# RWKV-7 scan on one NeuronCore: every product of the chunked scan in a 64x64 cell of the array

## The reference

```python
def step(s, inp):
    r_t, w_t, k_t, v_t, a_t, b_t = inp
    sa = jnp.einsum('bhij,bhj->bhi', s, a_t)
    s = s * w_t[:, :, None, :] + sa[..., None] * b_t[:, :, None, :] + v_t[..., None] * k_t[:, :, None, :]
    return s, jnp.einsum('bhij,bhj->bhi', s, r_t)
```

## Time and profile before

| | |
|---|---|
| median of three runs | 2237.53 us |
| profiled execution, span | 2236.4 us |
| PE, PEld busy | 2129.4 us (95%), 1368.9 us (61%) |
| DVE, ACT, POOL busy | 1177.5 (53%), 774.6 (35%), 647.4 us (29%) |
| granted TensorE clock, mean | 0.983 |

### The profile page before, as it was taken

How to read it: one execution, slowest core, us unless ns; L and a number is a source line. 1 busy time by engine, 2 the same in 40 slices (tenths; PEclk the granted TensorE clock), 3 DMA queues, 4 the chain that set the end, 5 groups by cost and what they waited for, 6 DMA issues and landing times. The chain is left out here.

```text
span 2236.4 us, 56049 instructions
## 1 busy us (share of the span) xinstructions
PE 2129.4 (95%) x23756; PEld 1368.9 (61%) x23756; DVE 1177.5 (53%) x2284; ACT 774.6 (35%) x2065; POOL 647.4 (29%) x901
## 2 busy tenths in 40 slices
PE   7999999999999999999896999999999999999798
PEld 3556565354444455444345888888888888888443
DVE  5443343134946770042624666666666666666674
ACT  4111111143255522210113444444444444444332
POOL 1010010023033410011123545444545444444011
PEclk9999999999999999999997999999999999999899
DMA  9201003701037766555314334533333333333742
GB/s 353 79 19 38 19 19 122 273 29 38 31 95 191 208 167 188 163 169 195 127 57 123 91 95 119 139 92 94 93 93 92 97 90 101 86 102 73 231 118 110
DMA packets 315866, 258.17 MB, mean 115 GB/s; under 512 B 138849, under 2 KB 272225, under 8 KB 312162
## 3 DMA queue, kind: packets, MB, share of 16 engines
q1 hardware_dynamic: 315618, 254.59, 37.9%
HBM read 174.80 MB, written 79.69 MB: 114 GB/s over the span
## 5 line engine op out<-in xcount | busy, mean ns | idle before, releaser
L1019 PE MATMUL ps<-xt,w_slab 128*128 128x512 f32 (+1 forms) x800 | 297.5, 526 | 0.0
L2168 PE MATMUL ps<-M,AT 64*64 64x64 f32 x6400 | 264.2, 224 | 7.6 <-ACT M L1957 4.4
L1883 POOL TENSOR_TENSOR SP<-Q,decay 64x128 f32<-64x128 f32 x304 | 128.7, 423 | 428.1 <-DVE Q L2086 399.6
L2168 PEld LDWEIGHTS ps<-M,AT 64*64 64x64 f32 x6400 | 219.3, 135 | 46.5 <-issue 14.6
L1019 PEld LDWEIGHTS ps<-xt,w_slab 128*128 128x128 f32 x800 | 148.3, 190 | 146.3 <-issue 122.6
L2168 PE MATMUL ps<-TT,MT 64*64 64x64 f32 x5120 | 215.6, 223 | 8.5 <-DVE TT L2029 1.3
L2168 PEld LDWEIGHTS ps<-TT,MT 64*64 64x64 f32 x5120 | 178.0, 135 | 39.6 <-issue 30.3
L2029 DVE COPY_PREDICATED TT<-mask,ps 128x128 f32<-128x128 int32 x400 | 125.1, 319 | 91.0 <-PE ps L2168 85.3
L2075 DVE STREAM_TRANSPOSE MT<-M 128x256 f32<-128x256 f32 x240 | 106.1, 442 | 125.8 <-ACT M L1957 123.8
L2161 PE MATMUL ps<-ar,bk 64*128 64x192 f32 (+1 forms) x1280 | 142.4, 342 | 14.3 <-POOL ar L1901 14.3
L645 PE MATMUL ps<-h,fgo 128*128 128x512 f32 x320 | 141.6, 597 | 2.4 <-PEq L202 2.4
(11 more groups left out here) (291 smaller groups left out, 3592.3 us busy)
## 6 DMA issues: line engine op xcount, KB each, us to landing
feat<-feature_scratch SPq DMA_DIRECT2D x160, 256.0 KB, 3.2
feature_scratch<-k_feats SPq DMA_DIRECT2D x64, 320.0 KB, 5.2
feature_scratch<-k_feats SPq DMA_DIRECT2D x24, 640.0 KB, 6.8
k_feats<-in_modw SPq DMA_DIRECT2D x8, 1536.0 KB, 6.7
w_slab<-in_rwin SPq DMA_DIRECT2D x24, 512.0 KB, 6.9
Q<-v_token_scratch SPq DMA_DIRECT2D x320, 32.0 KB, 2.5
Z<-v_token_scratch SPq DMA_DIRECT2D x320, 32.0 KB, 2.4
fgo<-in_modw SPq DMA_DIRECT2D x8, 1024.0 KB, 8.2
```

The source lines that it names most:

```text
L1019: mm = pe.matmul(ps[:, bank, 0:n], (w1t if i is None else w[:, i % 2])[:, k, :], src[:, k, a:a + n], start=k == 0, stop=k == KT - 1)
L1883: g.tensor_tensor(SP[own(h)], turn(sub, Q[l][own(h), h]), pend_turn(c, own(h), sub).unsqueeze(2).broadcast_to([HD, NDIR, CK]), ALU.mult).t ...
L2168: mm = pe.matmul(out[o, b, :], L[o, b, :], R[o, b, :], start=True, stop=True)
```

## The change

The reference's arithmetic stays. Every matmul of the scan becomes 64 rows by 64 columns. A cell whose rows and columns belong to one head is an "own" place; one whose rows are of one head and whose columns (output partitions) are of the other is a "crossed" place. The array has two of each.

- `products`: for each block four matmuls, two own (keys b against a, identity, r: tile `NG`, bank 0) and two crossed (keys k against the same: tile `XG`, bank 1), instead of two of 128 columns. ScalarE copies the own part (`first_n`), VectorE masks the crossed part (`first_x`) and the r columns (`first_r`), once per direction; products(1) waits for the copies of products(0).
- The values' products (`v_of_a`, `v_of_k`, `v_of_r`) run on the crossed places, for the following half-step, placed between the own matmuls of `a_state`, `r_state` and `sa`; the own products add onto them in PSUM later (`start=False`).
- Values are loaded four times a chunk rather than eight, into one tile V; the state has its own tile S; GpSimd scales and VectorE adds it in one instruction of 128 partitions rather than two of 64. GpSimd writes the a operand once instead of twice.
- The lists are reordered: TensorE does a_state, r_state, m4, products(0), sa, t8, b_state, y, m8, products(1), a_state, r_state, t16, sa, t2, m16, b_state, y, m2, t32, t4, mt32. On ScalarE the copy of sa(1) now stands behind that of m16, and the copy of products(0) ahead of that of sa(0).

```diff
-    RBK, BKt, Q, Z = ([sb(f"{n}{l}", [P, 2, B4, CK]) for l in range(SETS)] for n in ("RBK", "BKt", "Q", "Z"))
+    ar, NG, XG = ([sb(f"{n}{l}", [P, B4, 3, CK]) for l in range(SETS)] for n in ("ar", "NG", "XG"))
+    V = [sb(f"V{l}", [P, B4, CK]) for l in range(SETS)]
...
+            def first_n(j, cc, d):
+                act.wait_ge(pa, count("first", j, cc, PA[f"g{d}"]))
+                act.activation(gout(NG[lng(cc)], d, 0, 2), gall(0, 0, 2), ACT.Copy).then_inc(aa, 1)
...
+                if A_:
+                    first_n(j, c + 2, 0)
                 if Q_:
                     sa(j, c, 0)
-                if A_:
-                    first_at(j, c + 2)
                 if B_:
                     second(j, c + 1, "m8")
                 if A_:
-                    first_bk(j, c + 2)
+                    first_n(j, c + 2, 1)
                 if Q_ and is_lat(c):
                     y(j, c, 0)
                 if Q_:
                     r(j, c, 1)
-                    sa(j, c, 1)
                 if B_:
                     second(j, c + 1, "m16")
+                if Q_:
+                    sa(j, c, 1)
+                if A_:
+                    first_m2(j, c + 2)
...
+            def first_x(j, cc, d):
+                n = 3 if is_lat(cc) else 2
+                v.wait_ge(pa, count("first", j, cc, PA[f"g{d}"]))
+                v.tensor_tensor(gout(XG[lng(cc)], d, 0, n), gall(1, 0, n), xmask[d][:, 0:n * CK].unsqueeze(1).broadcast_to([P, 2, n * CK]), ALU.mult).then_inc(da, 1)
+
+            def first_r(j, cc, d):
+                v.wait_ge(aa, count("act_first", j, cc, AA[f"n{d}"]))
...
             def products(j, cc, d):
...
+                else:
+                    pe.wait_ge(aa, count("act_first", j, cc, AA["n0"]))
+                    pe.wait_ge(da, count("dve_first", j, cc, DA["x0"]))
...
                     for h in two:
                         o = own(h)
-                        mm = pe.matmul(gp(h, d, b)[:, cols[h], :], bk[s][o, 2 * d + b, :, :], ar[l][o, 2 * d + b, cols[h], :], start=True, stop=True)
+                        pe.matmul(gp(o, 0, b, n), bk[s][o, i, h, :], ar[l][o, i, 0:n, :], start=True, stop=True)
+                    for h in two:
+                        o = own(h)
+                        mm = pe.matmul(gp(other(h), 1, b, n), bk[s][o, i, 1 - h, :], ar[l][o, i, 0:n, :], start=True, stop=True)
...
+            def v_of_a(j, nx, d):
+                c, sub = nx
+                i = at(sub, d)
+                for h in two:
+                    pe.matmul(chain(sub, "r")[own(h), d, :], XG[lng(c)][other(h), i, 0, :], V[lng(c)][other(h), i, :], start=d == 0, stop=False, skip_group_check=True)
...
+            def a_state(j, c, sub):
+                nx = following(j, c, sub)
+                pe.wait_ge(dst, count("two", j, c, sub) + 1)
...
+                for d in range(NDIR):
+                    for h in two:
+                        o = own(h)
+                        mm = pe.matmul(chain(sub, "r")[o, d, :], ar[lng(c)][o, at(sub, d), 0, :], S[sub][o, d, :], start=False, stop=True, skip_group_check=True)
+                    if nx:
+                        v_of_a(j, nx, d)
                 mm.then_inc(pr, 1)
...
+            def b_state(j, c, sub):
+                pe.wait_ge(asa, count("two", j, c, sub + 1))
+                if not has_state((c, sub)):
+                    return
                 for d, h in pairs:
                     o = own(h)
+                    mm = pe.matmul(chain(sub, "st")[o, d, :], NG[lng(c)][o, at(sub, d), 1, :], SA[sub][o, d, :], start=False, stop=True, skip_group_check=True)
                 mm.then_inc(pst, 1)
```

More of the change, by code:

```diff
@@ L1878, in state_scaled @@
                 l = lng(c)
[L1879 to L1885, removed]
+                g.wait_ge(dst, count("two", j, c, sub) + 1)
+                g.tensor_tensor(SP[:], S[sub][:], pend_turn(c, slice(0, P), sub).unsqueeze(2).broadcast_to([P, NDIR, CK]), ALU.mult).then_inc(sp_ready, 1)
             def operands(j, cc):
@@ L2016, in _ @@
             v.wait_ge(tab_in, 16)
-            for h in two:
-                v.memset(turn(0, Q[0][own(h), h]), 0.0).then_inc(dst, 1)
+            v.memset(S[0][:], 0.0).then_inc(dst, 1)
             def masks():
@@ L2046, in first_m1 @@
                 v.transpose(flat(M[s]), flat(MT1[s][:])).then_inc(da, 1)
[L2048 to L2059, removed]
+            def first_x(j, cc, d):
[4 more added lines that the diff above has]
+                v.wait_ge(aa, count("act_first", j, cc, AA[f"n{d}"]))
+                v.tensor_tensor(gout(NG[lng(cc)], d, 2, 3), gall(0, 2, 3), xmask[d][:, 128:192].unsqueeze(1).broadcast_to([P, 2, CK]), ALU.mult).then_inc(drm, 1)
             def first_t(j, cc, k):
@@ L2205, in mt32, with following @@
                 pe.wait_ge(db, count("dve_second", j, cc, DB["t32"]))
-                level(lev(5), TT[32][s], MT[s], pb)
+                level(lev(5), TT[32][s], MT[trd(j, cc)], pb)
             def at(sub, d):
                 return 2 * d + (sub if d == 0 else 1 - sub)
-            def r(j, c, sub):
-                l = lng(c)
-                pe.wait_ge(dst, count("four", j, c, 2 * sub) + 2)
+            def following(j, c, sub):
                 if sub == 0:
-                    pe.wait_ge(ld_v[l], j * 256 + 128 + c // SETS * 128)
-                    pe.wait_ge(da, count("dve_first", j, c, DA["ak1"]))
-                for d, h in pairs:
-                    mm = pe.matmul(seq(6)[own(h), d, :], ar[l][:, at(sub, d), 3 * h, :], Q[l][:, h, at(sub, d), :], start=True, stop=True)
-                mm.then_inc(pr, 1)
+                    return (c, 1)
+                return (c + 1, 0) if j < KT - 1 or c + 1 < NCH else None
@@ new lines, in v_of_a, with v_of_k @@
+            def v_of_a(j, nx, d):
[3 more added lines that the diff above has]
+                    pe.matmul(chain(sub, "r")[own(h), d, :], XG[lng(c)][other(h), i, 0, :], V[lng(c)][other(h), i, :], start=d == 0, stop=False, skip_group_check=True)
+            def v_of_k(j, nx, d):
+                c, sub = nx
+                i = at(sub, d)
+                for h in two:
+                    mm = pe.matmul(chain(sub, "st")[own(h), d, :], XG[lng(c)][other(h), i, 1, :], V[lng(c)][other(h), i, :], start=False, stop=False, skip_group_check=True)
+                return mm
@@ new lines, in v_of_r, with v_ready, has_state @@
+            def v_of_r(j, nx, d):
+                c, sub = nx
+                i = at(sub, d)
+                for h in two:
+                    pe.matmul(ybank(sub)[own(h), d, :], XG[lng(c)][other(h), i, 2, :], V[lng(c)][other(h), i, :], start=d == 0, stop=False, skip_group_check=True)
+            def v_ready(j, cc):
+                pe.wait_ge(ld_v[lng(cc)], j * 128 + (cc // NCH * 128 + 64 + cc % NCH // SETS * 64))
+                pe.wait_ge(da, count("dve_first", j, cc, DA["x1"]))
+            def has_state(nx):
+                return nx != (NCH - 1, 1)
@@ L2221, in sa, with r_state @@
+            def r_state(j, c, sub):
+                nx = following(j, c, sub)
+                for d in range(NDIR):
+                    if is_lat(c):
+                        for h in two:
+                            o = own(h)
+                            pe.matmul(ybank(sub)[o, d, :], ar[lng(c)][o, at(sub, d), 2, :], S[sub][o, d, :], start=False, stop=False, skip_group_check=True)
+                    if nx and has_state(nx):
+                        v_of_k(j, nx, d)
             def sa(j, c, sub):
+                nx = following(j, c, sub)
@@ L2224, in sa @@
                     pe.wait_ge(ab, count("act_second", j, c, AB["xt"]))
-                ge(pe, ay, count("y", j, c, sub if is_lat(c) else 0))
+                ride = nx and is_lat(nx[0])
+                if ride:
+                    last = nx[0] - 1
+                    ge(pe, ay, count("y", j, last, nx[1] + 1 if is_lat(last) else 0))
+                for d in range(NDIR):
+                    for h in two:
+                        o = own(h)
+                        mm = pe.matmul(chain(sub, "sa")[o, d, :], MT[trd(j, c)][o, at(sub, d), :], Rs[sub][o, d, :], start=False, stop=True, skip_group_check=True)
+                    if ride:
+                        v_of_r(j, nx, d)
@@ L2250, in y @@
-            def y(j, c, sub):
-                l = lng(c)
-                for d, h in pairs:
-                    mm = pe.matmul(seq(7)[own(h), d, :], RBK[l][:, h, at(sub, d), :], Z[l][:, h, at(sub, d), :], start=False, stop=True, skip_group_check=True)
+                    mm = pe.matmul(ybank(sub)[o, d, :], NG[lng(c)][o, at(sub, d), 2, :], SA[sub][o, d, :], start=False, stop=True, skip_group_check=True)
                 mm.then_inc(py, 1)
@@ L2260, in period @@
                 if Q_:
-                    r(j, c, 0)
+                    a_state(j, c, 0)
+                    r_state(j, c, 0)
                 if B_:
```

197 lines of the change are left out of this document (94 added, 103 removed).

## The result

The changed kernel takes 2224.06 us (median of 6 runs) against 2237.35 us for the kernel before on the same chip: ratio 0.9947, 95% interval 0.9928 to 0.9965, so 13 us less (8 to 16). The direction was forecast; the size was not: 39 us were forecast. The profiled execution has a span of 2221.9 us, 14.5 less than before.

A forecast was written before the change was run, and what follows sets the result against it. TensorE was taken as the bound: the latent period falls from 11.24 to 10.65 us (8.29 matmuls plus 2.36 waits and stops). 28 us from 48 periods and 11 from 32 give 2198 us; range 2135 to 2250.

The forecast's parts named there:

- Shapes: TensorE, latent period: with all cells 64x64, twelve shape changes of 0.15 us go, 1.80 us less.
- Four places at no cost: TensorE: crossed products run beside own ones, adding 0 us per latent period, between bounds of 0 and 2.68.
- Rival A: TensorE: own and crossed places of the same rows take turns; latent period 12.19 us, total 2309, slower; chance 10%.
- Waits up to sa(1): Latent period walked from a_state at 0 to sa(1) at 5.59 to 5.87 us, with waits at m4 and b_state.
- the two waits of b_state: TensorE idles before b_state for sa's copy on ScalarE: 0.35 us in the first half, 0.70 in the second.
- B: ScalarE's copies queue at full length without overlap; latent period 11.43 us, total 2253; chance 12%.
- C: Shape-change drains go and waits stay at 1.15 us; latent period 9.44, total 2103; chance 8%.
- mt1 5.30, m1 0.44 later for 0.45: t2 starts at 6.24: VectorE's chain ahead of TensorE's t2: m1 follows mt1, so t2 starts at 6.24 us after a 0.37 wait.
- At nothing. GpSimd loses instructions: GpSimd's part was taken to cost nothing: it works a period ahead at under half load.
- 28 were forecast: Gain over the 48 periods with c = 2 to 7, like the one walked: 0.58 us each, 28 us.
- the 32 periods that were not walked: Periods that touch the context, mean before 10.71 us; 11 us of gain taken for them.
- The 0.35 for the others: Gain per period for the 32 not walked: the middle between 0.1 and 0.58 us.

The follow-up runs named there:

- e5: Changed kernel with products put back into cells of 64 rows by 128 columns (one head's data wrong): latent period 10.88 us.
- e4: Changed kernel without the 24 value products on the crossed places (values' part left out of the result): 2215.7 us, latent period 10.86.
- e3: Changed kernel with sa(1)'s copy on ScalarE ahead of m16's copy, as in the kernel before: 2182.50 us, latent period 10.11.
- e2: Changed kernel with GpSimd's list reordered so that no operand product runs beside mt1: 28 us gained, latent period 10.63.
- e7: Changed kernel with NG by kind, GpSimd's operand products kept off mt1, and several ScalarE and VectorE copies moved ahead: 2172 us.
- e8: e7 with the last projection's weights loaded in 64 pieces over all head pairs: 6 us off e7, 0.968 of the kernel before.
- e11: e3 with the crossed value products all issued but moving one column instead of 64: 2181.75 us.

## Why the prediction was wrong

- **Shapes: right.** No gap of 0.15 is left; 0.85 became 0.65 at products, and e5 brings 0.85 back.
- **Four places at no cost (taken at 0 of 2.68): right.** Four records start per 0.058 us; e4's period is the same without the crossed ones. Rival A did not happen, nor did weight loads wait for matmuls of their own rows.
- **Waits up to sa(1): right** within 0.04 us, the two waits of b_state with them. B did not happen (R starts 0.17 after M in the changed kernel too), nor C (e3 shows that the 0.70 was the moved copy).
- **The step that failed: "mt1 5.30, m1 0.44 later for 0.45: t2 starts at 6.24".** mt1's duration was carried over from the row of before, where it met only GpSimd's scaling of the state. It measured 0.67 in the latent periods walked and 0.77 to 0.98 in the usual ones of the others, since GpSimd's products now run beside it. The cause lies in the part **"At nothing. GpSimd loses instructions"**: it was asked whether GpSimd would be late, not what its earlier start would collide with. state(0) comes 3.5 us into the period (4.9 before), and with it the scaled state and all of GpSimd's products behind it.
- **The size.** The measured 2224 us lies inside the stated range; what failed is the size of the gain. By the usual periods 48 x 0.37 = 18 us came where 28 were forecast, and 1 us where 11 were taken for the 32 periods that were not walked. Without the meeting the change is worth 43 us by the usual periods (e2), and 39 were forecast. The 0.35 for the others was a guess; without the meeting they gain 0.44 on average. The meeting costs 8 x 3.0 = 24 us: 0.24 in each of the 48 periods walked, and more in the 32 others, where 0.2 (c = 0, 1), 0 (c = 8) and -0.2 (c = 9) came out. The waits for issue cost some 4 more.
- **Not in the prediction at all: TensorE's instruction supply.** 25% more instructions in a shorter period bring stalls of about 1 us. In e7 the total falls by 65 us where its shortest periods promise 8 x 14.7 = 118.

## What to carry to other kernels

When an edit lets an engine start earlier, list what will now run beside each operation of the chain, not only what will be late: a duration read from a row holds for the company it had there. Splitting matmuls over more places of the array costs no time on TensorE, but it costs instructions, and they have a supply of their own. Before adding up gains of a reordering, walk every engine's list in order: a copy placed one position too late (e3) outweighed the gain of the whole change.

## What the runs showed of the hardware

- Four 64x64 places of TensorE run f32 matmuls side by side, 0.058 us per four records of 64 columns, with own and crossed places in different PSUM banks.
- VectorE's masked copy of 128x256 f32 from SBUF takes 0.44 us alone and 0.67 to 0.98 beside GpSimd's products of 128x256; of these the a product grows from 0.69 to 0.85 itself, the bk products stay at 0.73. Beside GpSimd's scaling of the state on 64 partitions the copy took 0.41 in the kernel before. VectorE's product from PSUM (first_x) stays at 0.56 beside them. The Trainium skill, SBUF — State Buffer, Who interferes with whom, says that a VectorE instruction with two SBUF inputs contends with a GpSimd instruction that reads SBUF; e2 agrees (0.73 to 0.44), the 0.41 beside the scaling of the state does not.
- TensorE got no more than about 61 records per us in the mean of 350 us (e7, e8), whether the crossed matmuls moved 64 columns or one (e11); 50 us of e7 reached 65. Its pauses end 1.2 to 1.7 us after a 16 KB piece of its instructions has landed (114 of 114). Spreading 4 MB of weight loads (e8) shortened the second head pair by 8 us and the whole by 6, so other traffic has a part in it, but most pauses stay when that traffic is spread.
